# Two of the modulation's 24 column groups summed by TensorE instead of VectorE, with six slots for their pieces, and the first two groups of the output projection in turn

## The chip, the cores and the metric

One core of a Trainium2 chip runs the whole program. The metric is the device time of one execution in microseconds; the median of several runs is compared.

## The reference

Two decoder layers over a sequence of 256 tokens of width 2048, in f32 (`DEPTH` 2, `SEQ` 256, `D_FF` 5632). Each layer takes a modulation vector from `c`:

```
mod = (c_act @ ada_w[layer] + ada_b[layer])[:, None, :]
sh_m, sc_m, g_m, sh_f, sc_f, g_f = jnp.split(mod, 6, axis=-1)
h = rmsnorm(x, norm_mix[layer]) * (1 + sc_m) + sh_m
x = x + g_m * mix
h = rmsnorm(x, norm_ffn[layer]) * (1 + sc_f) + sh_f
x = x + g_f * swiglu(h, ffn_w_gate[layer], ffn_w_up[layer], ffn_w_down[layer])
```

In layer 0, `mix` is a projection of `h` to 5632 columns (`w_in`), 12 heads of dilated attention and four groups of a spatial gating unit (SGU) on it, and an output projection (`w_out`) of the 16 pieces. In layer 1 it is a short gated convolution between two projections. A final RMSNorm ends it.

`ada_w` is 2 x 2048 x 12288 f32. The product with it is a vector times a matrix: each of its 384 pieces of 512 KB is read once and used for one row of the result.

## The kernel before, in words

**Units.** All wide products run in 388 units: 0 to 43 the input projection, 44 to 59 the output projection, 60 to 191 the FFN of layer 0, then the convolution's and the second FFN. A unit is a 512x512 block of a weight matrix for both halves of the tokens: 24 matmuls of 512 columns. The weights come as two pieces of 512 KB (`raw`, slots: `RAW`). ScalarE rounds a piece to `whi` (L437), VectorE makes `wlo` = raw - whi (L730), and TensorE multiplies three times, high x whi, high x wlo, low x whi (`half_unit`, L1108 to L1110). There are four `whi`/`wlo` slots (`SPLIT`): ScalarE and VectorE work on the pieces of unit u+2 while TensorE runs unit u. The four banks 0 to 3 of PSUM hold the sums of two groups of units.

**The modulation.** `ADA` lists 24 groups of 1024 columns; the first four are quarters, 512 columns of shift and 512 of scale each. A group is 16 steps, one piece of `ada_w` each (128 rows, 1024 columns). In a step VectorE adds piece x `cact[:, k]` into one of two accumulators `acc` (`ada_op`, L756, for the first step L752, or L745 ahead of it); the 128 partitions are then summed by TensorE with a matrix of ones. For a shift or a scale that is `reduce_cols` (L1136), eight matmuls of one column with a 128x128 tile of `acc` as weights, and VectorE adds the bias (`keep_cols`). For a gate it is `reduce_row` (L1145).

**Order.** Every engine has its own queue in program order. `ada_to(u)` says up to which step the sum has come behind unit u: SyncE issues unit u+2's raw pieces and then that unit's ada pieces on one queue (`load_ada`, L367; `load_piece`, L354), and each load of ada waits until the step four before it has been done (`ADA_SLOTS`). VectorE runs the steps of unit u (`ada_ops`) behind the two `lo_piece` of that unit. The quarters are reduced behind units 8, 14 and 20 (`REDUCE_AT`), the other groups where `ADA_REDUCE` puts them. Behind a quarter, two blocks of the normalised x are transposed and scaled (`norm_turn`, `norm_quarter`), which the next part of the input projection needs: `VISITS` cuts that projection by quarters of its depth, so that its sums are kept in SBUF and added to by VectorE (`add_visit`, L912).

**Heads.** Between units 26 and 46, TensorE also runs the turns, scores and products of the heads (`SCORE_UNIT`, `QK_TURNS`); `heads_out` and `head_lo` put head m into `mixed` four units behind its scores. Units 44 and 45 take pieces 0 to 7 of `mixed` for the first group of output columns, unit 46 the SGU's pieces (waits for `sg_ready`), unit 47 the heads 8 to 11 (waits for `o_ready`); then the second, third and fourth group of columns follow, four units each. Each of these lines is in `OUT_ORDER` and at the end of the tensor block:

```
unit(46, G_OUT, 2, 4, mixed, sg_ready, lambda t: 2, 12)
heads_out(46)
reduce_ada(46)
unit(47, G_OUT, 3, 4, mixed, o_ready, lambda t: HEADS, 8)
```

Behind unit 59 the norm ahead of the FFN is made, whose shift and scale are the groups 6 to 9.

Of the kernel before, what the change touches and what calls it, by code (L numbers as in the profile page):

```python
# [37 lines left out]
RAW = 6  # L38
SPLIT = 4
ADA_SLOTS = 4  # L40
# [16 lines left out]
VISIT_AT = {u: v for u, (v, c, k) in enumerate(IN_UNITS) if k == VISITS[v][1][-1]}  # L57
LAST = {c: v for v, (c, ks) in enumerate(VISITS)}
BEFORE = {v: max((w for w in range(v) if VISITS[w][0] == c), default=None) for v, (c, ks) in enumerate(VISITS)}
KEPT = {c: n for n, c in enumerate((0, 3, 1, 4, 2, 5, 9, 10))}  # L60
UNIT_OF = {v: u for u, v in VISIT_AT.items()}
FIRST_OF = {k: min(u for u in range(44) if IN_UNITS[u][2] == k) for k in range(4)}
# [9 lines left out]
GROUP_END = [sum(GROUP_UNITS[:g + 1]) - 1 for g in range(len(GROUP_UNITS))]  # L72

# [11 lines left out]
ADA_OPS = KT * len(ADA)  # L85

ANGLES_AT, TRIG_AT = 3, 5
REDUCE_AT = {8: 1, 14: 2, 20: 3}
# [6 lines left out]
ROWS_TO = [sum(is_row(i) for i in range(j)) for j in range(len(ADA) + 1)]  # L95
COLS_TO = [j - ROWS_TO[j] for j in range(len(ADA) + 1)]
RED_TO = [j + ROWS_TO[j] for j in range(len(ADA) + 1)]


def cols_done(layer, which, n):  # L100
    return COLS_TO[ADA.index((layer, which, n))] + 1


def rows_done(layer, which, n):
    return 2 * ROWS_TO[ADA.index((layer, which, n))] + 2

# [44 lines left out]
TURNS = [[(t, q) for q in range(4) for t in range(2)]] + 4 * [((0, 0), (0, 1), (1, 0), (1, 1), (0, 2), (1, 2), (0, 3), (1, 3))]  # L151

SCORE_UNIT = (28, 29, 30, 33, 34, 35, 36, 37, 38, 39, 41, 42)
SCORE_AT = {u: n for n, u in enumerate(SCORE_UNIT)}
QK_TURNS = ((26, 0, 0, 0), (28, 0, 1, 0), (27, 0, 0, 1), (29, 0, 1, 1), (30, 1, 0, 0), (32, 1, 1, 0),
            (34, 1, 0, 1), (35, 1, 1, 1), (36, 2, 0, 0), (37, 2, 1, 0), (38, 2, 0, 1), (40, 2, 1, 1))
QK_TURNS = tuple(sorted(QK_TURNS))
QK_AT = {u: [b for b, q in enumerate(QK_TURNS) if q[0] == u] for u in range(46)}  # L160
QK_INDEX = {q[1:]: b for b, q in enumerate(QK_TURNS)}

# [5 lines left out]

OUT_ORDER = ((0, 1, 3, 2), (0, 1, 2, 3))
# [19 lines left out]
def decoder_kernel(nc, x_in, c_col, pos, ada_w, ada_b, g_mix, g_ffn, w_in, sgu_w, sgu_b, w_out,  # L191
                   conv_in, conv_w, conv_out, ff_gate, ff_up, ff_down, g_fin, freq_in, ident_in,
                   mask_in, out):
    with ExitStack() as ctx:
# [49 lines left out]
        junk = sb("junk", [P, 2, COLS], mybir.dt.bfloat16)  # L244
# [26 lines left out]
        Q_BANK, S_BANK, P_BANK, O_BANK, ADA_BANK = 4, 5, 6, 7, 7  # L271

# [7 lines left out]
        ada_step, ada_init, red_done, mod_done, row_done = sems("ada_step ada_init red_done mod_done row_done")  # L280
# [15 lines left out]
        N_CONST = 10  # L296

# [27 lines left out]
        def weight_pieces():  # L325
# [4 lines left out]
            for n in range(4):  # L330
                for k in OUT_ORDER[n > 0]:
                    for half in range(2):
                        yield piece_of(w_out_v, 2 * k + half, n)
# [14 lines left out]
        def _(sp):  # L348
# [7 lines left out]
            def load_ada(a):  # L356
                layer, which, n = ADA[a // KT]
                if a >= ADA_SLOTS:
                    sp.wait_ge(ada_step, a - ADA_SLOTS + 1)
                to, w = ada[:, a % ADA_SLOTS], ada_v[layer, :, a % KT, :]  # L360
                if a < QUARTERS * KT:
# [32 lines left out]
        def _(pool):  # L394
            def rope(i, kind):
                n = 2 * i + kind
                c = (Q, K)[kind][i]
                freed(pool, LAST[c], 0)
                freed(pool, LAST[c], 1)
# [11 lines left out]

            nc.gpsimd.memset(ones[:, :], 1.0).then_inc(pool_const, 1)
# [5 lines left out]
            for i in range(3):  # L418
                for kind in range(2):
                    rope(i, kind)  # L420
            for r, (g, n, t, on_ve) in enumerate(RES):
                if not on_ve:
                    freed(pool, g, t)
                    xs = x[:, t, COLS * n:COLS * n + COLS]
                    nc.gpsimd.tensor_tensor(xs, xs, tmp[:, r % 2, :], ALU.add).then_inc(x_pool, 1)  # L425
# [3 lines left out]
        def _(sa):  # L429
# [13 lines left out]
            def keep_row(u):  # L443
                for j, n in ADA_AT[u]:
                    if is_row(j):
                        half = ADA[j][2]
                        gate = ROWS_TO[j] // 2
# [3 lines left out]
                        sa.wait_ge(red_done, RED_TO[j] + n + 1)  # L451
# [35 lines left out]
            def norm_scaled(k, i, layer, sh):  # L487
# [122 lines left out]
            for n in range(46):  # L610
# [14 lines left out]
                for c in (SG_V, SG_U):  # L625
                    if n == UNIT_OF[LAST[c]] + 1:
                        freed(sa, LAST[c], 0)
                        freed(sa, LAST[c], 1)
# [36 lines left out]
            for n in range(2, 15):  # L665
# [61 lines left out]
        def _(ve):  # L727
# [9 lines left out]
            def ada_op(a):  # L737
                j, k = a // KT, a % KT
                layer, which, n = ADA[j]
                to, src, c = acc[:, j % 2, :], ada[:, a % ADA_SLOTS, :], cact[:, k:k + 1]  # L740
                if k == 0 and j >= 2:
                    ve.wait_ge(red_done, RED_TO[j - 1])
                if k == 0 and is_row(j):
# [5 lines left out]
                    ve.wait_ge(ada_init, ROWS_TO[j] + 1)  # L749
# [3 lines left out]
                else:  # L753
                    if k:
                        ve.wait_ge(ada_step, a)
# [7 lines left out]
            def keep_cols(j):  # L763
                layer, which, n = ADA[j]
                ve.wait_ge(red_done, RED_TO[j] + 1)
                if j < QUARTERS:
                    to, src = (v[:, :].rearrange("p (w f) -> p w f", f=KT)[:, SH_M:SC_M + 1, 4 * n:4 * n + 4]
                               for v in (mod, adab))
                    nc.vector.tensor_tensor(to, ps[:, ADA_BANK, COLS - 8:COLS].rearrange("p (w f) -> p w f", w=2), src,
                                            ALU.add).then_inc(mod_done, 1)  # L770
                else:
                    col = mod_column(layer, which, 8 * n)
# [656 lines left out]
```

## Time and profile before

| | |
|---|---|
| median of 3 runs | 2384.12 us (2381.06 to 2386.44) |
| the profiled execution | 2381.44 us, of it 2379.7 us from its first to its last instruction |
| TensorE (PE) busy | 2265.2 us, 95% |
| VectorE (DVE) busy | 1643.3 us, 69% |
| ScalarE (ACT) busy | 1056.7 us, 44% |
| DMA | 615.89 MB, mean 259 GB/s |
| mean granted clock of TensorE | 0.985 |

The profile's times are microseconds from the span's start. "Idle before, releaser" is the time an engine stood still ahead of an instruction, and what ended it. PEclk is the granted clock as a share of 2.4 GHz; 0.50 is the lower of its two levels, 1.2 GHz. The table of windows gives the busy time of each engine and, in brackets, its instructions.

### The profile page before, as it was taken

To read this page: it belongs to the slowest core of one execution; us is meant where nothing else is said; L and a number is where in the kernel's file an instruction comes from. 1 tells how busy PE (TensorE), PEld (TensorE's weight loads), DVE (VectorE), ACT (ScalarE), POOL (GpSimd) and SP (SyncE) were. 2 spreads that over 40 slices of the span, in tenths; PEclk is the share of its full clock that TensorE was granted. 3 is DMA by queue.
4 is the path that set the end of the run, shared out by engine and by line. 5 is a ranking of instruction groups with operands and counts; after the bars stand their busy time and mean duration, and the time that the engine had idled before them with its cause. 6 is when DMAs were issued, how large, how long until landed. Compare 5 with 4: busy or idle time off the path is not lost.

```text
span 2379.7 us, 26483 instructions
## 1 busy us (share of the span) xinstructions
PE 2265.2 (95%) x10172; PEld 1868.3 (79%) x10172; DVE 1643.3 (69%) x1618; ACT 1056.7 (44%) x1333; POOL 106.7 (4%) x71
## 2 busy tenths in 40 slices
PE   3988898989999999999999999998999999999998
PEld 2776677778888888888887888887888888888886
DVE  5898998977766777667777777687774454444554
ACT  4533454364444334444446444446444443444443
POOL 0002210100000010000010000010000001000010
PEclk9999999989999999999999999999999999999999
DMA  8897898968888888888886888886886666666663
GB/s 315 324 324 266 311 323 304 351 240 290 277 267 289 276 280 294 278 273 282 278 283 224 272 280 270 278 280 216 305 272 179 194 188 194 194 191 189 188 192 124
DMA packets 277838, 615.89 MB, mean 259 GB/s; under 512 B 19792, under 2 KB 20176, under 8 KB 277328
## 3 DMA queue, kind: packets, MB, share of 16 engines
q1 hardware_dynamic: 276272, 613.50, 77.4%
q8 instruction: 81, 1.33, 0.2%
q10 hardware_dynamic: 1440, 0.69, 0.1%
q14 instruction: 45, 0.37, 0.0%
HBM read 612.02 MB, written 2.10 MB: 258 GB/s over the span
## 4 chain that ended last, share of the span: by engine, by line
PE 81%; DVE 11%; issue 3%; DMA 3%; ACT 2%; SPq 0%; DVEq 0%; ACTq 0%
PE ps L1108 26%; PE ps L1109 26%; PE ps L1110 26%; DVE acc L756 5%; DVE wlo L730 3%; PE ps L1158 2%; DMA ada<-ada_w 2%; PE ps L1136 1%; DMA raw<-w_in 1%; DMA raw<-w_out 1%; ACT whi L437 1%; ACT hf L497 1%; DVE kept L912 1%; PE ps L1145 0%; DVE vtok L912 0%
## 5 line engine op out<-in xcount | busy, mean ns | idle before, releaser
L730 DVE TENSOR_TENSOR wlo<-raw,whi 128x1024 fp32r<-128x1024 f32 x776 | 957.6, 1237 | 645.5 <-ACT whi L437 645.4
L437 ACT ACTIVATE whi<-raw 128x1024 fp32r<-128x1024 f32 x776 | 823.2, 1062 | 1225.3 <-PE ps L1110 1053.2
L1108 PE MATMUL ps<-whi,h 128*128 128x512 f32 x2144 | 854.5, 399 | 21.9 <-issue 8.5
L1109 PE MATMUL ps<-wlo,h 128*128 128x512 f32 x2144 | 839.9, 392 | 0.0
L1110 PE MATMUL ps<-whi,h 128*128 128x512 f32 x2144 | 839.8, 392 | 0.0
L756 DVE SCALAR_TENSOR_TENSOR acc<-ada,cact,acc 128x1024 f32<-128x1024 f32 x368 | 486.4, 1322 | 23.0 <-DMA ada<-ada_w 12.2
L1108 PEld LDWEIGHTS ps<-whi,h 128*128 128x128 f32 x2144 | 406.1, 189 | 113.1 <-issue 18.9
L1109 PEld LDWEIGHTS ps<-wlo,h 128*128 128x128 f32 x2144 | 406.3, 190 | 85.4 <-issue 3.8
L1110 PEld LDWEIGHTS ps<-whi,h 128*128 128x128 f32 x2144 | 405.6, 189 | 86.2
L1108 PE MATMUL ps<-whi,act 128*128 128x512 f32 x704 | 274.7, 390 | 0.0
L1110 PE MATMUL ps<-whi,act 128*128 128x512 f32 x704 | 274.0, 389 | 0.0
L1109 PE MATMUL ps<-wlo,act 128*128 128x512 f32 x704 | 273.9, 389 | 0.0
L425 POOL TENSOR_TENSOR x<-x,tmp 128x512 f32<-128x512 f32 x40 | 70.8, 1793 | 1962.1 <-DVE tmp L847 1962.1
L1110 PEld LDWEIGHTS ps<-whi,act 128*128 128x128 f32 x704 | 132.1, 188 | 27.5
L1109 PEld LDWEIGHTS ps<-wlo,act 128*128 128x128 f32 x704 | 132.2, 188 | 27.3
L1108 PEld LDWEIGHTS ps<-whi,act 128*128 128x128 f32 x704 | 132.2, 188 | 27.2
L1108 PE MATMUL ps<-whi,mixed 128*128 128x512 f32 x256 | 103.7, 405 | 10.7 <-DVE wlo L730 5.4
L1109 PE MATMUL ps<-wlo,mixed 128*128 128x512 f32 x256 | 102.3, 400 | 0.0
L1110 PE MATMUL ps<-whi,mixed 128*128 128x512 f32 x256 | 102.0, 398 | 0.0
L1108 PEld LDWEIGHTS ps<-whi,mixed 128*128 128x128 f32 x256 | 49.7, 194 | 22.8 <-DVE wlo L730 7.1
L1158 PE MATMUL ps<-ident,xn 128*128 128x128 f32 x128 | 21.5, 311 | 42.6 <-ACT xn L484 42.6
L1110 PEld LDWEIGHTS ps<-whi,mixed 128*128 128x128 f32 x256 | 49.7, 194 | 10.8
(113 smaller groups left out, 842.5 us busy)
## 6 DMA issues: line engine op xcount, KB each, us to landing
ada<-ada_w SPq DMA_DIRECT2D x384, 512.0 KB, 5.6
raw<-ff_gate SPq DMA_DIRECT2D x176, 512.0 KB, 4.1
raw<-ff_up SPq DMA_DIRECT2D x176, 512.0 KB, 3.8
raw<-ff_down SPq DMA_DIRECT2D x176, 512.0 KB, 4.2
raw<-conv_in SPq DMA_DIRECT2D x96, 512.0 KB, 4.5
raw<-w_in SPq DMA_DIRECT2D x88, 512.0 KB, 6.8
raw<-w_out SPq DMA_DIRECT2D x32, 512.0 KB, 7.0
raw<-conv_out SPq DMA_DIRECT2D x32, 512.0 KB, 5.2
```

Of the source, the lines that this page charges most:

```text
L425: nc.gpsimd.tensor_tensor(xs, xs, tmp[:, r % 2, :], ALU.add).then_inc(x_pool, 1)
L437: nc.scalar.activation(whi[v % SPLIT][:, :, :], raw[:, v % RAW], ACT.Copy).then_inc(hi_ready, 1)
L497: nc.scalar.activation(hfs[k][:, i % 3, P * m:P * m + P], ps[:, 4 + i % 3, P * m:P * m + P], ACT.Identity, bias=mod[:, col:col + 1], scale ...
L730: nc.vector.tensor_tensor(wlo[v % SPLIT][:, :, :], raw[:, v % RAW], whi[v % SPLIT][:, :, :].bitcast(F32), ALU.subtract).then_inc(lo_ready, 1)
L756: nc.vector.scalar_tensor_tensor(out=to, in0=src, scalar=c, in1=to, op0=ALU.mult, op1=ALU.add)\
L912: nc.vector.tensor_tensor(of, ps[:, acc_bank(v, t), :], of, ALU.add).then_inc(acc_free[acc_bank(v, t)], 1)
L1108: nc.tensor.matmul(to, high, whi[v % SPLIT][:, k, :], start=begin, stop=False)
L1109: nc.tensor.matmul(to, high, wlo[v % SPLIT][:, k, :], start=False, stop=False)
L1110: ins = nc.tensor.matmul(to, low, whi[v % SPLIT][:, k, :], start=False, stop=end)
L1136: ins = nc.tensor.matmul(ps[:, ADA_BANK, COLS - 8 + n:COLS - 7 + n], acc[:, j % 2, P * n:P * n + P], ones[:, 0:1], start=True, stop=True)
L1158: return nc.tensor.transpose(to, src, ident[:, :])
```

## The change

The lines below are the core of the diff. `PE_GROUPS` are group 3 (the last quarter) and group 9 (the second half of the shift for layer 0's FFN).

```
-RAW = 6
+RAW = 5
-ADA_SLOTS = 4
+ADA_SLOTS = 6
+OUT_UNITS = ([(n, k) for ks in ((0, 1), (3, 2)) for n in range(2) for k in ks]
+             + [(n, k) for n in range(2, 4) for k in range(4)])
+PE_GROUPS = (3, 9)
+PE_LAG = 1
-REDUCE_AT = {8: 1, 14: 2, 20: 3}
+REDUCE_AT = {9: 1, 15: 2, 21: 3}
 def ada_to(u):
-    if u < 22:
-        return min(4 * KT, KT + (12 * (u + 1)) // 5)
+    if u < 9:
+        return 16 + 16 * (u + 1) // 9
+    if u < 21:
+        return 32 + 32 * (u + 1 - 9) // 12
     if u < U_F0 - 2:
-        return min(10 * KT, 4 * KT + (14 * (u - 21)) // 5)
-    return min(ADA_OPS, 10 * KT + u - (U_F0 - 3))
+        return min(10 * KT, 64 + 96 * (u + 1 - 21) // 36)
+    return min(len(OPS), 10 * KT + u - (U_F0 - 3))
...
+TURN_BANKS = ((5, 6), (4, 5, 6), (4, 5, 6), (4, 5, 6))
...
-        junk = sb("junk", [P, 2, COLS], mybir.dt.bfloat16)
+        junk = sb("junk", [P, COLS], mybir.dt.bfloat16)
...
+        def summed(engine, a):
+
+            j, k = OPS[a]
+            if j not in PE_GROUPS:
+                engine.wait_ge(ada_step, KT * VE_INDEX[j] + k + 1)
+            elif k < KT - 1:
+                engine.wait_ge(pe_step, (KT - 1) * PE_GROUPS.index(j) + k + 1)
+            else:
+                engine.wait_ge(red_done, RED_INDEX[j, 0] + 1)
...
             def load_ada(a):
-                    sp.wait_ge(ada_step, a - ADA_SLOTS + 1)
+                    summed(sp, a - ADA_SLOTS)
...
             def ada_op(a):
+                if j in PE_GROUPS:
+                    return
...
+            def ada_sums(u):
+
+                for a in range(ada_to(u - 1), ada_to(u)):
+                    j, k = OPS[a]
+                    if j not in PE_GROUPS:
+                        continue
+                    to = ps[:, SUM_BANK[j], 0:8]
+                    if k == 0:
+                        if j >= QUARTERS:
+                            pe.wait_ge(sg_ready, 2)
+                        nc.tensor.matmul(to, ident[:, :], columns_of(adab, j), start=True, stop=False)
+                    pe.wait_ge(ada_loaded[a % ADA_SLOTS], 16 * (a // ADA_SLOTS + 1))
+                    for n in range(8):
+                        ins = nc.tensor.matmul(to[:, n:n + 1], ada[:, a % ADA_SLOTS, P * n:P * n + P],
+                                               cact[:, k:k + 1], start=False, stop=k == KT - 1 and n == 7)
+                    ins.then_inc(red_done if k == KT - 1 else pe_step, 1)
...
             pe.wait_ge(const_loaded, 16 * N_CONST)
             norm_turn(0, 0)
+            reduce_cols(0)
             norm_turn(0, 1)
-            reduce_cols(0)
...
+            def out_unit(n):
+                m, k = OUT_UNITS[n]
+                ks = [q for i, q in OUT_UNITS if i == m]
+                ready, value = None, HEADS
+                if m == 0:
+                    ready = sg_ready if k == 3 else o_ready
+                    value = 2 if k == 3 else 4 * k + 4
+                unit(U_OUT + n, G_OUT + m, ks.index(k), 4, mixed, ready, lambda t: value, 4 * k)
...
+                ada_sums(n - PE_LAG)
```

A step of group 3 or 9 is now eight matmuls with a 128x128 tile of the piece itself as weights and one column of `cact` moving, added up in PSUM on top of the bias; no accumulator and no reduction follow, and VectorE only copies the eight columns. TensorE runs the steps of unit u behind unit u+1. Group 3 lies behind units 15 to 20, group 9 behind units 51 to 56. Of `SBUF`, one raw slot and one buffer of `junk` are given up for two ada slots. In the output projection, units 44 to 51 are now groups 0, 0, 1, 1, 0, 0, 1, 1, the SGU's pieces in unit 48 and the heads 8 to 11 in unit 49. The norm's first eight transposes use two banks instead of three. Steps done behind unit 20 are 64 in both; behind unit 28 they are 83 before and 85 now, behind unit 45 131 and 130, behind unit 50 145 and 144.

The first place is VectorE at units 15 to 18 (each line of `wlo` ends one half of a unit's work; `acc<-ada,cact,acc` are modulation steps). Before:

```order
L756 SCALAR_TENSOR_TENSOR acc<-ada,cact,acc 128x1024 x2
L730 TENSOR_TENSOR wlo<-raw,whi 128x1024
L912 TENSOR_TENSOR vtok<-ps,vtok 128x512 x2
L730 TENSOR_TENSOR wlo<-raw,whi 128x1024
L756 SCALAR_TENSOR_TENSOR acc<-ada,cact,acc 128x1024 x2
L730 TENSOR_TENSOR wlo<-raw,whi 128x1024
```

Now:

```order
L854 TENSOR_TENSOR h<-hf_51,h 128x4x128 x2
L779 TENSOR_TENSOR wlo<-raw,whi 128x1024
L953 TENSOR_TENSOR kept<-ps,kept 128x512 x2
L779 TENSOR_TENSOR wlo<-raw,whi 128x1024 x2
L953 TENSOR_TENSOR kept<-ps,kept 128x512 x2
L779 TENSOR_TENSOR wlo<-raw,whi 128x1024 x2
```

The steps between the `wlo` are gone; the additions of the visits (L953) stay.

The second place is TensorE (PE) behind unit 16, the end of its wide matmuls (L1158, L1159) and what stands ahead of unit 17, in the kernel now:

```order
L1158 MATMUL ps<-wlo,h 128x512
L1159 MATMUL ps<-whi,h 128x512
L1208 MATMUL ps<-adab,ident 128x8
L1211 MATMUL ps<-cact,ada 128x1 x16
L1227 MATMUL ps<-ident,xn_49 128x128 x8
L1157 MATMUL ps<-whi,h 128x512
```

The bias comes first (L1208), then the sixteen one-column matmuls of two steps. Before, unit followed unit there, and the one-column matmuls of a reduction stood once, behind unit 14:

```order
L1109 MATMUL ps<-wlo,h 128x512
L1110 MATMUL ps<-whi,h 128x512
L1136 MATMUL ps<-ones,acc 128x1 x8
L1108 MATMUL ps<-whi,h 128x512
L1109 MATMUL ps<-wlo,h 128x512
```

The third place is SyncE's queue at the start. Before:

```order
L369 DMA cact<-c_col 128x16
L367 DMA ada<-ada_w 128x2x512 x4
L372 DMA x<-x_in 128x2x2048
L367 DMA ada<-ada_w 128x2x512 x12
L354 DMA raw<-w_in 128x2x512 x6
```

Now:

```order
L411 DMA cact<-c_col 128x16
L409 DMA ada<-ada_w 128x2x512 x6
L414 DMA x<-x_in 128x2x2048
L409 DMA ada<-ada_w 128x2x512 x10
L395 DMA raw<-w_in 128x2x512 x6
```

Two more pieces stand ahead of x.

## Rows read from the trace of the kernel before

**Rows 1.** The page, part 1: busy time, share, instructions.

```profile
PE 2265.2 (95%) x10172; PEld 1868.3 (79%) x10172; DVE 1643.3 (69%) x1618; ACT 1056.7 (44%) x1333; POOL 106.7 (4%) x71
```

**Rows 2.** Windows, the rest of the span; columns as in rows 3.

```profile
495.00:2379.70 1884.70, 1859.05 (x8360) 1536.79 (x8360) 1224.41 (x1155) 835.20 (x977) 60.25 (x34) 0.99 0.75 244
```

**Rows 3.** Windows: width, busy PE, PEld, DVE, ACT, POOL, then PEclk, DMA share, GB/s.

```profile
45.80:99.80 54.00, 53.85 (x233) 44.07 (x233) 45.42 (x49) 31.03 (x45) 0.00 (x0) 1.00 0.87 312
99.80:147.30 47.50, 38.41 (x171) 30.89 (x170) 41.38 (x42) 22.60 (x32) 0.00 (x0) 0.96 0.94 340
147.30:194.10 46.80, 39.08 (x169) 32.10 (x170) 41.94 (x44) 17.18 (x23) 0.00 (x0) 0.90 0.91 317
194.10:255.80 61.70, 50.42 (x217) 40.32 (x218) 51.12 (x49) 23.50 (x30) 22.77 (x16) 0.94 0.73 256
255.80:393.00 137.20, 126.92 (x619) 104.25 (x617) 132.28 (x180) 76.88 (x150) 12.08 (x9) 0.99 0.91 318
393.00:429.90 36.90, 34.81 (x141) 28.98 (x142) 26.90 (x24) 9.99 (x13) 3.53 (x2) 0.86 0.77 272
429.90:468.70 38.80, 36.55 (x162) 29.70 (x160) 35.50 (x31) 13.97 (x16) 3.50 (x2) 0.96 0.99 376
468.70:499.70 31.00, 22.61 (x97) 17.79 (x97) 23.96 (x28) 14.61 (x25) 3.52 (x2) 0.87 0.85 316
```

**Rows 4.** PE in order of time: start, duration, line, idle before.

```profile
143.82 3.58 PE L1136 MATMUL ps<-ones,acc 128*128 128x1 f32 x16 [4.61 <-DVE acc L756]
...
190.69 3.57 PE L1136 MATMUL ps<-ones,acc 128*128 128x1 f32 x16 [6.02 <-DVE acc L756]
...
392.95 0.80 PE L1108 MATMUL ps<-whi,mixed 128*128 128x512 f32 x1 [5.27 <-DVE mixed L995]
...
400.05 0.59 PE L1235 MATMUL ps<-probT,vtok 128*128 128x256 f32 x2
...
402.95 3.45 PE L1136 MATMUL ps<-ones,acc 128*128 128x1 f32 x16 [2.09 <-DVE mixed L894]
...
486.75 0.49 PE L1108 MATMUL ps<-whi,mixed 128*128 128x512 f32 x1
```

**Rows 5.** DMA between 430 and 440 us.

```profile
DMA packets 1543, 4.05 MB, mean 405 GB/s; under 512 B 127, under 2 KB 127, under 8 KB 1543
```

**Rows 6.** PE, wide matmuls at full clock, and the eighth and ninth after 406.26.

```profile
774.21 0.39 PE L1108 MATMUL ps<-whi,h 128*128 128x512 f32 x1
774.43 0.39 PE L1109 MATMUL ps<-wlo,h 128*128 128x512 f32 x1
...
409.40 0.63 PE L1109 MATMUL ps<-wlo,mixed 128*128 128x512 f32 x1
409.82 0.46 PE L1110 MATMUL ps<-whi,mixed 128*128 128x512 f32 x1
```

**Rows 7.** The page, part 5: all of VectorE's modulation steps; busy, mean ns.

```profile
L756 DVE SCALAR_TENSOR_TENSOR acc<-ada,cact,acc 128x1024 f32<-128x1024 f32 x368 | 486.4, 1322 | 23.0 <-DMA ada<-ada_w 12.2
```

**Rows 8.** PE, one reduction at full clock, and wide matmuls behind reductions.

```profile
774.89 1.84 PE L1136 MATMUL ps<-ones,acc 128*128 128x1 f32 x16
776.59 0.49 PE L1108 MATMUL ps<-whi,act 128*128 128x512 f32 x1
...
147.26 0.77 PE L1108 MATMUL ps<-whi,h 128*128 128x512 f32 x1
...
406.26 0.77 PE L1108 MATMUL ps<-whi,mixed 128*128 128x512 f32 x1
```

**Rows 9.** DVE at the start, the step behind the load of x.

```profile
17.91 1.28 DVE L756 SCALAR_TENSOR_TENSOR acc<-ada,cact,acc 128x1024 f32<-128x1024 f32 x1 [5.50 <-DMA ada<-ada_w]
```

**Rows 10.** Windows at the start, columns as in rows 3.

```profile
24.00:28.00 4.00, 0.00 (x0) 0.00 (x0) 3.41 (x3) 0.00 (x0) 0.00 (x0) 1.00 0.87 275
```

**Rows 11.** Waits between 194 and 256 us: total, times, longest.

```profile
ACT whi L437 <- DMA raw<-w_in: 27.9, 10, 6.7
```

**Rows 12.** Windows around the fall of the clock, columns as in rows 3.

```profile
402.00:403.00 1.00, 0.05 (x1) 0.05 (x1) 0.90 (x2) 0.00 (x0) 0.00 (x0) 1.00 1.02 406
403.00:404.00 1.00, 1.00 (x6) 1.00 (x6) 0.00 (x0) 0.00 (x0) 0.00 (x0) 0.56 0.52 211
```

More of the change, by code:

```diff
@@ L296, in decoder_kernel, with columns_of, kept_of, whole @@
         N_CONST = 10
+        def summed(engine, a):
[6 more added lines that the diff above has]
+                engine.wait_ge(red_done, RED_INDEX[j, 0] + 1)
+        def columns_of(v, j):
+            layer, which, n = ADA[j]
+            if j < QUARTERS:
+                return v[:, :].rearrange("p (w f) -> p w f", f=KT)[:, SH_M:SC_M + 1, 4 * n:4 * n + 4]
+            col = mod_column(layer, which, 8 * n)
+            return v[:, col:col + 8]
+        def kept_of(c, t):
+            return kept[:, KEPT[c], t, :] if c in KEPT else vtok[:, t, COLS * (c - 6):COLS * (c - 5)]
+        def whole(engine, c):
+            for t in range(2):
+                freed(engine, LAST[c], t)
         def freed(engine, g, t):
@@ L329, in weight_pieces @@
                     yield piece_of(w_in_v, 2 * k + half, c)
[L330 to L333, printed above, removed]
+            for n, k in OUT_UNITS:
+                for half in range(2):
+                    yield piece_of(w_out_v, 2 * k + half, n)
             yield from feed_pieces(0)
@@ L417, in _ @@
             pool.wait_ge(trig_ready, 4)
[L418 to L425, printed above, removed]
+            for u in range(U_F0):
+                for i in range(3):
+                    for kind in range(2):
+                        if UNIT_OF[LAST[(Q, K)[kind][i]]] == u:
+                            rope(i, kind)
+                for r, (g, n, t, on_ve) in enumerate(RES[:8]):
+                    if not on_ve and GROUP_END[g] == u:
+                        residual(r)
+            for r in range(8, len(RES)):
+                if not RES[r][3]:
+                    residual(r)
         @block.scalar
@@ L669, in _ @@
                 keep_row(U_OUT + n)
-                if n % 4 == 1 and n > 4:
-                    square(R_OUT + 2 * (n // 4) - 2)
-                    square(R_OUT + 2 * (n // 4) - 1)
+                for m in range(3):
+                    if n == OUT_LAST[m] + 2:
+                        square(R_OUT + 2 * m)
+                        square(R_OUT + 2 * m + 1)
             norm(1, 0, SH_F, U_F0)
@@ L748, in ada_op @@
                         .then_inc(ada_init, 1)
-                    ve.wait_ge(ada_init, ROWS_TO[j] + 1)
+                    ve.wait_ge(ada_init, sum(is_row(i) for i in range(j)) + 1)
                 ve.wait_ge(ada_loaded[a % ADA_SLOTS], 16 * (a // ADA_SLOTS + 1))
@@ L895, in head_lo, with add_visit @@
                                             ALU.subtract).then_inc(o_ready, 1)
+            def add_visit(v):
+                for t in range(2):
+                    of = kept_of(VISITS[v][0], t)
+                    ve.wait_ge(acc_done, 2 * v + t + 1)
+                    freed(ve, BEFORE[v], t)
+                    nc.vector.tensor_tensor(of, ps[:, acc_bank(v, t), :], of, ALU.add).then_inc(acc_free[acc_bank(v, t)], 1)
             def gain_quarter(q):
@@ L1232, in heads_out @@
                     pe.wait_ge(mod_done, QUARTERS + cols)
-                    for t in range(2):
-                        freed(pe, LAST[V[m // 4]], t)
+                    whole(pe, V[m // 4])
                     nc.tensor.matmul(ps[:, O_BANK, 0:S], vtok[:, 0, P * m:P * m + P], probT[:, m % 2, 0:S],
@@ L1254, in _ @@
                 else:
-                    unit(n, G_OUT, n - 44, 4, mixed, o_ready, lambda t: 4 * (n - 44) + 4)
-                if n in REDUCE_AT:
+                    out_unit(n - 44)
+                ada_sums(n - PE_LAG)
+                if n in REDUCE_AT and REDUCE_AT[n] not in PE_GROUPS:
                     reduce_cols(REDUCE_AT[n])
```

180 lines of the change are left out of this document (93 added, 87 removed).

## The prediction

> **What bounds the kernel now.** I read the page first, then the table of eight stretches, then the instructions in order at the places where TensorE (PE) stood still, then the waits. Over the whole span PE is busy 95% [rows 1], and from 495 us on it has no hole worth naming: 1859 of 1884.7 us busy [rows 2]. There only a change of PE's own work could tell. The 500 us before are another kernel. I cut them where units of the first two projections begin, a unit being 24 wide matmuls, counted from the first at 45.84 us: units 0 to 8, 9 to 14, 15 to 20, 21 to 28, 29 to 45, 46 to 50, 51 to 56, and 57 to 59 with the norm's start [rows 3]. VectorE (DVE) is busy 41.4 of 47.5, 41.9 of 46.8 and 132.3 of 137.2 us there, PE 38.4, 39.1 and 126.9: both are nearly full, and DVE is what PE waits for. It waits 4.61, 6.02 us for a step of the modulation sum, and 5.27 and 2.09 us in units 46 and 47 for the last pieces of `mixed` [rows 4]. DMA moves 256 to 376 GB/s in these stretches; a window of 10 us shows 405 [rows 5]. So there are three resources, each within a fifth of the next.
>
> A wide matmul follows the one before by 0.227 us, so a unit is 24 x 0.227 = 5.44 us; at the clock's lower level (0.50) it follows by 0.42 to 0.43 [rows 6].
>
> **What the change moves.** 32 of the 160 modulation steps of this part (groups 3 and 9) leave DVE, at 1.322 us each [rows 7]: 42.3 us. PE takes each as eight one-column matmuls on a 128x128 f32 tile. No such accumulating run is in the trace, but the reduction of a summed group has the same shape: eight of them took 1.84 us at full clock and the next wide matmul began 1.70 us after their start; at half clock 3.44 us (143.82 to 147.26) [rows 4, 8]. I take 1.70 us: 16 x 1.70 = 27.2 us a group, 54.4 together, less two reductions (3.4) that fall away. Bounds of one step: nothing excludes that the sixteen loads overlap the wide matmul ahead better, which the 0.106 us between passes caps at some 1.5; above, 3.44.
>
> Where this lies matters more than the total. The order shows group 3 behind units 15 to 20 and group 9 behind units 51 to 56, two or three steps each time. There a PE unit becomes 5.44 + 2.67 x 1.70 = 10.0 us on the mean, while DVE is left with two `wlo` and at most two additions.
>
> Stretch by stretch, against the profiled run (481 us and the rest by its own span 2379.7, its time 2381.44):
> - *Start, to 45.84.* DVE stood 5.50 us for a piece behind x [rows 9] and 0.5 to 1.4 us four times more, 3.8 together, at 275 GB/s where 405 are to be had [rows 5, 10]. Six slots instead of four let SP issue two pieces more before x, and ask two steps earlier after it. I take 5 us off (0 to 8: all the stalls).
> - *Units 0 to 8.* PE is full. One reduction moves on to unit 9: -1.7.
> - *Units 9 to 14.* DVE's work is 41.4 plus one step, 42.7 against 47.5: -4.8.
> - *Units 15 to 20.* PE: 6 x 5.44 + 27.2 + 1.7 (a reduction) + 1.6 (sixteen transposes, an estimate from the sizes: 128 columns each, f32 twice, 0.1 us) = 63.1 against 46.8: +16.3.
> - *Units 21 to 28.* The new pace puts 21 steps here where 19 were, DVE 51.1 + 2.6 = 53.7, and I leave 2.3 of its 10.6 idle us: 56.0 against 61.7, -5.7. The idle hung on loads: ScalarE waited 27.9 us for `w_in` [rows 11]. SP is one queue, and a load of ada waits for the step four before it; with six slots that wait lies further back. Five slots of raw instead of six take a little of it away.
> - *Units 29 to 45.* DVE, 45 steps instead of 48: -3.9, and some 2 of waits: -6.
> - *Units 46 to 50.* With two groups in turn, the SGU pieces come in unit 48 and the last heads in unit 49, so the 5.27 and the 2.09 us and the half clock behind each go. Left is 5 x 5.44 + 1.8 (two heads, 0.9 each as at 400.05 [rows 4]) + 1.7 = 30.7 on PE, and 24 loads of 512 KB at 405 GB/s, 31.1: 31.5 against 36.9, -5.4.
> - *Units 51 to 56.* 6 x 5.44 + 27.2 + 1.7 = 61.5 against 38.8: +22.7.
> - *Units 57 to 59.* DVE and loads have had 20 us of slack, so PE runs through: 16.3 + the 7.5 us that the norm adds behind unit 59 (it began at 486.75 [rows 4], and 499.7 - 486.75 - 5.44 = 7.5) = 23.8 against 31.0: -7.2.
> - *After 499.7.* 328 units on PE; the raw loads come in early enough that no wait for them is in the list there, one slot less or not: 0.
>
> Sum: -5 -1.7 -4.8 +16.3 -5.7 -6 -5.4 +22.7 -7.2 = +3.2 us. DVE's 42 us and the slots buy 36, and PE takes 39. Cover: in both PE blocks the loads for the next units are hidden by PE; what is late next is PE itself.
>
> **The clock.** One term is missing. Behind a reduction at half clock the clock stayed at half: the passes ran from 402.95, the wide matmuls from 406.26, and still the eighth and the ninth of these stood 0.42 us apart, at 409.40 and 409.82, the ninth the first short one [rows 4, 6]. And it fell at 403, some 3 us after the wide matmuls had ended, though heads' matmuls stood in between [rows 4, 12]. A lone run of 1.84 us leaves it at full [rows 6, 8]. The new runs are 3.4 us (four) and 5.1 us (eight). If the clock falls in one, a last step costs 1.7 more and eight wide matmuls behind it 8 x 0.2 = 1.6: 3.3 us a fall. I take four of the twelve, half of the long ones: +13.2. Bounds 0 and 12 x 3.3 = 40.
>
> The Trainium skill, "TensorE: Matmul & The Clock Gate", Part 1, says that the throttled state is the default and that only array activity releases it, and Part 4 that transposes don't count as busy in the same way. Read that way, one-column passes, which are nearly all weight load, would not hold the clock in any of the runs; the trace agrees for the runs that began at half clock, and has none longer than 1.84 us that began at full. By the rule the sum would be +43, by the rows alone anything from +3.
>
> Forecast: 3.2 + 13.2 = +16.4 on the median of the runs, 2384.12 (the profiled run is 2.7 under it): 2400.5 us.
>
> **Rivals.**
> *PE's holes pay for it (faster).* In the eight stretches from 45.8 to 499.7 PE is busy 402.7 of 453.9 us: 51.2 are idle, exactly what the new work needs (54.4 - 3.4), and cold starts add some 12. If buffers (two units of wlo, six of ada, five of raw) let PE's full blocks and DVE's full blocks overlap, as they do if each engine can run two units off, all of it is filled: -12 - 5 at the start = -17, of which I take 15, 2369 us. It decides where units 21 to 50 take under 200 us in place of my 56.0 + 131.2 + 31.5 = 218.7. For: so many waits are for DVE or loads. Against: a DVE that ran ahead has only four whi/wlo slots, two units.
> *The clock falls in every run (slower still).* +3.2 + 40 = 2427 us. From what is said above.
> *A wash.* No fall at all, and +3.2: 2387 us; the reordering and the two buffers pay for PE's blocks.
> *The change doesn't do what it says:* excluded by the order rows; the steps are gone from DVE and the one-column matmuls are there.
> *Group 9 late.* Its columns (the shift of the next norm) are ready in unit 57, before the norm needs them behind unit 59; a fall on this needs PE to be 10 us behind its own order, which can't be. No chance given.
>
> **How the numbers follow.** Some clock falls, +10 to +25: 0.38. All or nearly all: 0.14. Wash, within 5 us: 0.18. Holes pay: 0.30. A change of 0.2% (4.8 us) is about what a measurement of this kernel can tell from none. Faster 0.30; same 0.16 (most of the wash); slower 0.54 (the first two and the rest of the wash). The range holds from the rival's 2369 to the all-falls 2427, with 2 us on the low side left in for noise of the median: 2367 to 2427. The likeliest case by itself is 2392 to 2410.
>
> **What would show it.** Right: PE units of about 10 us at 15 to 20 and 51 to 56, DVE idle there, one-column runs at 1.70 us a step, granted clock at 0.50 in parts of them; first wide matmul near 41; no 5 us hole in unit 46; start of the FFN near 503 plus the falls; from there the same 1880 us. Wrong: a step under 1.3 us on PE, the clock at 1.0 all through both blocks, or units 21 to 50 in less than 205 us.

## The result and the profile after

The changed kernel takes 2441.3 us (median of 4 runs, 2438.82 to 2442.1) against 2382.59 for the kernel before on the same chip: a ratio of 1.0244, 95% interval 1.0226 to 1.0262, 58.7 us slower. The profiled execution took 2440.86 us, 2439.1 of them its span. The forecast was slower, 2400.5, with a range up to 2427: the direction was right, the size was not, and the measured time lies outside the range.

The page, part 1, after (engine, busy us, share, instructions), against [rows 1]:

```profile
PE 2346.8 (96%) x10656; PEld 1946.6 (80%) x10656; DVE 1604.9 (66%) x1586; ACT 1058.4 (43%) x1333; POOL 106.7 (4%) x71
```

VectorE is busy 38 us less (the forecast moved 42.3), and TensorE 82 us more. The same stretches as in [rows 3], cut at the starts of the same units. Columns: stretch, width, busy time of PE, PEld, DVE, ACT, POOL, then PEclk, DMA share, GB/s.

```profile
0.00:42.90 42.90, 5.61 (x24) 4.84 (x24) 22.87 (x25) 15.99 (x33) 1.08 (x7) 1.00 0.90 324
42.90:94.30 51.40, 51.38 (x216) 42.13 (x217) 42.40 (x47) 33.33 (x47) 0.00 (x0) 1.00 0.96 348
94.30:137.30 43.00, 38.83 (x170) 31.51 (x170) 34.07 (x35) 20.66 (x29) 0.00 (x0) 0.92 0.93 323
137.30:221.80 84.50, 76.76 (x380) 67.13 (x378) 34.16 (x38) 18.53 (x24) 0.00 (x0) 0.76 0.60 202
221.80:288.10 66.30, 61.23 (x267) 50.66 (x267) 49.10 (x48) 23.72 (x30) 17.05 (x12) 0.87 0.77 260
288.10:421.30 133.20, 125.05 (x617) 102.25 (x615) 128.94 (x175) 73.71 (x149) 17.87 (x12) 1.00 0.93 324
421.30:451.10 29.80, 29.80 (x143) 24.97 (x141) 29.07 (x30) 10.87 (x13) 2.64 (x2) 1.00 0.98 366
451.10:523.00 71.90, 71.52 (x372) 63.11 (x371) 29.48 (x25) 16.45 (x21) 7.84 (x5) 0.80 0.74 252
523.00:558.70 35.70, 29.21 (x130) 24.23 (x130) 12.91 (x19) 12.61 (x23) 0.00 (x0) 0.79 0.36 118
558.70:2439.10 1880.40, 1857.38 (x8352) 1535.79 (x8352) 1221.88 (x1150) 832.55 (x969) 60.23 (x34) 0.99 0.75 244
```

| stretch | before | after | difference | forecast |
|---|---|---|---|---|
| start | 45.8 | 42.9 | -2.9 | -5 |
| units 0 to 8 | 54.0 | 51.4 | -2.6 | -1.7 |
| 9 to 14 | 47.5 | 43.0 | -4.5 | -4.8 |
| 15 to 20 | 46.8 | 84.5 | +37.7 | +16.3 |
| 21 to 28 | 61.7 | 66.3 | +4.6 | -5.7 |
| 29 to 45 | 137.2 | 133.2 | -4.0 | -6 |
| 46 to 50 | 36.9 | 29.8 | -7.1 | -5.4 |
| 51 to 56 | 38.8 | 71.9 | +33.1 | +22.7 |
| 57 to 59 and the norm's start | 31.0 | 35.7 | +4.7 | -7.2 |
| the rest | 1880.0 | 1880.4 | +0.4 | 0 |

The forecast column leaves out the clock, for which 13.2 us stood beside it. Read the PEclk column: it is 0.76 and 0.80 in the two stretches with the new work, 0.90 and 0.96 before. A unit with three steps behind it now takes 14.4 us; with 1.70 us a step it would be 5.44 + 5.10 = 10.5. These windows hold one such unit each:

```profile
181.90:196.30 14.40, 14.40 (x74) 12.68 (x74) 3.74 (x4) 2.12 (x2) 0.00 (x0) 0.74 0.47 160
483.20:497.60 14.40, 14.40 (x74) 12.81 (x74) 2.45 (x2) 2.12 (x2) 0.00 (x0) 0.74 0.61 190
```

PE is busy for the whole of them and VectorE for about a quarter or less. The clock falls inside the run of one-column passes. The run behind unit 21 began at 228.92, without a hole:

```profile
231.00:232.00 1.00, 1.00 (x11) 1.00 (x11) 0.43 (x1) 0.00 (x0) 0.00 (x0) 1.00 0.55 74
232.00:233.00 1.00, 1.00 (x7) 1.00 (x7) 0.00 (x0) 0.00 (x0) 0.00 (x0) 0.53 0.68 229
...
236.00:237.00 1.00, 1.00 (x4) 0.90 (x4) 0.64 (x3) 0.00 (x0) 0.00 (x0) 0.50 0.95 350
```

From 232 on 6 to 7 passes a us go through instead of 11, and the wide matmuls from 236.15 on start at the lower level too.

So it is in all eight runs of three steps. The four runs of two steps went through at full clock, some 3.5 us for both steps, and there the clock fell within 0.5 us of the run's end, in one of them 1.2 us behind it, in the one-column reduction that followed. One of the twelve falls, the one behind unit 16 at 163.8, may not be the steps' doing: without any group on TensorE (next section) the clock falls near the same place, at about 164. Every run of steps began at full clock.

ScalarE and VectorE now stand still for TensorE, which has not yet given back the `whi` and `wlo` of an earlier unit. Up to the FFN's first unit, before (0 to 500) and after (0 to 560), in total, times, longest:

```profile
ACT whi L437 <- PE ps L1110: 65.4, 28, 9.4
```

```profile
ACT whi L487 <- PE ps L1159: 230.3, 84, 13.3
```

### The profile page after: what moved, and what is told of

Its sections match the earlier page's. It is cut to its first block, busy times and chain, and to the rows that moved or that the text cites. A ratio compares the mean times of both kernels' runs of the same rounds, so it can differ in the third digit from the quotient of the medians.

```text
span 2439.1 us, 27386 instructions
## 1 busy us (share of the span) xinstructions
PE 2346.8 (96%) x10656; PEld 1946.6 (80%) x10656; DVE 1604.9 (66%) x1586; ACT 1058.4 (43%) x1333; POOL 106.7 (4%) x71
## 4 chain that ended last, share of the span: by engine, by line
PE 87%; DVE 8%; issue 3%; DMA 1%; ACT 1%; DVEq 0%; SPq 0%; ACTq 0%
PE ps L1157 27%; PE ps L1158 27%; PE ps L1159 27%; DVE acc L809 4%; PE ps L1211 3%; DVE wlo L779 2%; PE ps L1227 2%; PE ps L1189 1%; DMA ada<-ada_w 1%; DVE kept L953 0%; PE ps L1195 0%; DVE mx L1015 0%; ACT hf L547 0%; ACT whi L487 0%; DMA raw<-w_in 0%
## 5 line engine op out<-in xcount | busy, mean ns | idle before, releaser
L1158 PE MATMUL ps<-wlo,h 128*128 128x512 f32 x2144 | 845.3, 394 | 0.0
L1159 PE MATMUL ps<-whi,h 128*128 128x512 f32 x2144 | 844.6, 394 | 0.0
L1158 PEld LDWEIGHTS ps<-wlo,h 128*128 128x128 f32 x2144 | 409.4, 191 | 86.7 <-issue 3.8
L1159 PEld LDWEIGHTS ps<-whi,h 128*128 128x128 f32 x2144 | 408.8, 191 | 87.1
L809 DVE SCALAR_TENSOR_TENSOR acc<-ada,cact,acc 128x1024 f32<-128x1024 f32 x338 | 445.4, 1318 | 17.5 <-DMA ada<-ada_w 8.6
L1159 PE MATMUL ps<-whi,act 128*128 128x512 f32 x704 | 274.0, 389 | 0.0
L1158 PE MATMUL ps<-wlo,act 128*128 128x512 f32 x704 | 273.9, 389 | 0.0
L1159 PEld LDWEIGHTS ps<-whi,act 128*128 128x128 f32 x704 | 132.1, 188 | 27.6
L1158 PEld LDWEIGHTS ps<-wlo,act 128*128 128x128 f32 x704 | 132.2, 188 | 27.2
L1157 PE MATMUL ps<-whi,mixed 128*128 128x512 f32 x256 | 107.1, 418 | 0.4 <-DVE wlo L779 0.4
L1158 PE MATMUL ps<-wlo,mixed 128*128 128x512 f32 x256 | 104.9, 410 | 0.0
L1159 PE MATMUL ps<-whi,mixed 128*128 128x512 f32 x256 | 104.5, 408 | 0.0
L1211 PEld LDWEIGHTS ps<-cact,ada 128*128 128x128 f32 x512 | 70.4, 223 | 0.8
L1211 PE MATMUL ps<-cact,ada 128*128 128x1 f32 x512 | 69.5, 271 | 0.0
```

Of the source, the lines that this page charges most:

```text
L809: nc.vector.scalar_tensor_tensor(out=to, in0=src, scalar=c, in1=to, op0=ALU.mult, op1=ALU.add)\
L1157: nc.tensor.matmul(to, high, whi[v % SPLIT][:, k, :], start=begin, stop=False)
L1158: nc.tensor.matmul(to, high, wlo[v % SPLIT][:, k, :], start=False, stop=False)
L1159: ins = nc.tensor.matmul(to, low, whi[v % SPLIT][:, k, :], start=False, stop=end)
L1211: ins = nc.tensor.matmul(to[:, n:n + 1], ada[:, a % ADA_SLOTS, P * n:P * n + P], cact[:, k:k + 1], start=False, stop=k == KT - 1 and n == 7)
```

## The experiments

Every run was timed in three rounds against the kernel before on the same chip. The kernel before had medians of 2382.6, 2384.8, 2382.7 and 2382.4 us in the four sets, so a difference between runs of two sets is good to some 2 us.

### First set: take the parts apart

**No group on TensorE.** All else as changed.

```
-PE_GROUPS = (3, 9)
+PE_GROUPS = ()
```

> The changed kernel with no group on TensorE (PE_GROUPS empty): slots, pace, order of the output projection and reductions as changed, all 160 steps on VectorE. Theory A (the one-column runs, with the clock they lower, are the whole loss): the 12 long units go, and what is left are the gains of the slots and the order, 3 us at the start, 3 in units 0 to 8, 4 in units 29 to 45, 7 in units 46 to 50: about 2366 us, 2358 to 2376. Rival B (the pace, the slots or the later reductions cost something themselves): above 2390.

Measured: 2364.2 us, ratio 0.9921 (0.9901 to 0.9942). Theory A stands on this run, rival B falls: the 32 steps on TensorE cost 2441.3 - 2364.2 = 77.1 us, and the rest of the change gains 18.4.

**The steps spread.** The same 32 steps, one behind each quarter of a unit; `pe_step_of` is the body of `ada_sums` for one step.

```
 def unit(u, g, n, nu, of, ready=None, value=None, k0=None):
+    steps = pe_steps(u - PE_LAG)
     for half in range(2):
         for t in range(2):
...
             half_unit(u, g, t, n == 0, n == nu - 1, of, 4 * n if k0 is None else k0, half)
+            if steps:
+                pe_step_of(steps.pop(0))
```

> The changed kernel with the same steps on TensorE, but one at a time behind each quarter of a unit (1.7 us of one-column passes between 1.4 us of wide matmuls) instead of two or three in a row behind the unit. Theory A (only long unbroken runs lower the clock): granted clock 1.0 in the blocks, a unit 10.0 us on the mean instead of 14 with three steps, 12 units: 40 us less, about 2400 us. Rival C (what counts is the share of one-column work over a longer time, or the steps are slow for another reason, a wait for the pieces or the semaphores): the clock falls all the same, 2435 to 2445 or more.

Measured: 2406.4 us, ratio 1.0099 (1.0076 to 1.0122), 34.9 less than with the steps in a row. Two windows of two units with three steps each, and one step in order of time:

```profile
203.90:225.80 21.90, 21.90 (x147) 19.80 (x146) 7.67 (x8) 4.24 (x4) 0.00 (x0) 1.00 0.74 240
455.70:477.60 21.90, 21.90 (x147) 19.86 (x147) 5.14 (x6) 4.51 (x7) 0.00 (x0) 1.00 0.87 302
```

```profile
205.11 0.39 PE L1159 MATMUL ps<-whi,h 128*128 128x512 f32 x1
205.34 1.84 PE L1213 MATMUL ps<-cact,ada 128*128 128x1 f32 x16
207.04 0.49 PE L1157 MATMUL ps<-whi,h 128*128 128x512 f32 x1
```

The granted clock is 1.00 where it was 0.74, and two units with three steps each take 21.9 us instead of 28.8. The instructions are the same, so the 35 us are the clock's. The granted clocks say so too: 0.972 over 2439.1 us is some 68 us lost to the lower level, 0.987 over 2407.6 us some 31 (an estimate from spans and mean clocks). A step takes 1.70 us at full clock, as forecast; with the slower first wide matmul behind it a unit pays (10.95 - 5.44) / 3 = 1.84. Rival C falls as a forecast of this run; that the share of wide work counts is taken up in the third set. What is left, 2406.4 - 2364.2 = 42.2 us, is the price of the steps where the clock is mostly held.

Mostly, because in units 15 to 20 it was not. It had fallen at 147.4, in a hole of 5.53 us ahead of the reduction behind unit 15, and the first two spread steps began at the lower level:

```profile
148.78 3.58 PE L1195 MATMUL ps<-ones,acc 128*128 128x1 f32 x16 [5.53 <-DVE acc L809]
...
155.20 3.55 PE L1213 MATMUL ps<-cact,ada 128*128 128x1 f32 x16
...
161.32 3.41 PE L1213 MATMUL ps<-cact,ada 128*128 128x1 f32 x16
...
173.03 0.47 PE L1157 MATMUL ps<-whi,h 128*128 128x512 f32 x1 [3.10 <-issue]
```

The clock came back at 167.8, after 20.4 us, in the twelve wide matmuls that follow the second step. In the changed kernel, with 24 wide matmuls unbroken after the same reduction, it came back after some 10 (146.8 to 157.0). Six wide matmuls a step kept a full clock full; here, in the one case there is, they did not bring a low one back. The stretches from unit 15 on, cut at the starts of units 15, 21, 24, and of 51 and 58, the last to the FFN's first unit:

```profile
137.60:214.90 77.30, 68.67 (x380) 60.97 (x380) 33.13 (x36) 17.36 (x23) 0.00 (x0) 0.87 0.68 228
214.90:243.50 28.60, 24.30 (x130) 20.74 (x129) 19.70 (x22) 10.41 (x16) 0.00 (x0) 0.94 0.71 236
243.50:275.60 32.10, 30.23 (x140) 24.55 (x138) 31.07 (x29) 14.41 (x15) 17.06 (x12) 1.00 0.90 312
...
438.60:508.40 69.80, 69.41 (x443) 62.06 (x442) 31.37 (x26) 17.50 (x22) 6.92 (x5) 1.00 0.78 271
508.40:527.60 19.20, 13.03 (x57) 10.41 (x56) 11.59 (x18) 11.53 (x21) 0.00 (x0) 0.87 0.54 175
```

**The output projection's order alone**, on the kernel before: `OUT_UNITS`, `out_unit`, and the residuals and squares that hang on them, as in the change.

> The kernel before with only the output projection's first two groups in turn. Theory D (the waits of units 46 and 47 for the last heads and the SGU were on the path): 5.3 + 2.1 us of waits and some 3 us of half clock behind them go, 2374 to 2378 us. Rival E (VectorE is the bound there and only the place of the wait moves): within 2 us of before.

Measured: 2381.0 us, ratio 0.9993 (0.9984 to 1.0003): no difference that can be told, rival E. Unit 46 starts at 389.95 instead of 392.95, but until the next unit 15.6 us go by. The wait has only moved, to the reduction behind unit 46; the fourth set takes it away.

```profile
402.13 3.57 PE L1142 MATMUL ps<-ones,acc 128*128 128x1 f32 x16 [5.82 <-DVE mixed L899]
```

**The slots alone**, on the kernel before.

```
-RAW = 6
+RAW = 5
-ADA_SLOTS = 4
+ADA_SLOTS = 6
```

> The kernel before with only the slots changed: raw 5, ada 6, junk one buffer. Theory F (loads asked for earlier shorten the stalls on VectorE and ScalarE): 3 us at the start and 3 to 10 in units 9 to 45, 2370 to 2380 us. Rival G (one raw slot less makes up for it): within 2 us of before, or above.

Measured: 2369.8 us, ratio 0.9948 (0.9931 to 0.9966), 12.8 us less: theory F, at its upper end. ScalarE's waits for `w_in` between 194 and 256 us are 17.1 us instead of the 27.9 of [rows 11].

```profile
ACT whi L437 <- DMA raw<-w_in: 17.1, 6, 5.2
```

### Second set: where the 18 us come from, and the dear group

**Slots and order together**, on the kernel before.

> The kernel before with both the slots (raw 5, ada 6, one junk) and the output projection's first two groups in turn, nothing else. Alone they gave 12.8 us and 1.6 us. Theory H (the order only pays once the loads keep up: unit 45 to 51 took 31 to 44 us less in the run with everything but TensorE's groups): 2369.8 less 8 to 12, about 2359 us, under both kernels. Rival I (they add up as they stand, or share the same stalls): 2367 to 2371 us.

Measured: 2368.2 us, ratio 0.9934 (0.9919 to 0.9948). They do not add up to more than the slots: theory H falls.

**Early reductions.** The changed kernel with no group on TensorE, and the quarters' reductions of before together with the pace of the first 21 units that they need.

```
-    if u < 9:
-        return 16 + 16 * (u + 1) // 9
     if u < 21:
-        return 32 + 32 * (u + 1 - 9) // 12
+        return min(4 * KT, KT + (12 * (u + 1)) // 5)
...
-REDUCE_AT = {9: 1, 15: 2, 21: 3}
+REDUCE_AT = {8: 1, 14: 2, 20: 3}
```

> The changed kernel with no group on TensorE, and the pace of the first 21 units and the quarters' reductions as before (behind units 8, 14 and 20 instead of 9, 15 and 21). Theory J (a reduction one unit later leaves the norm's quarter no time before the unit that needs it, and PE waits at units 11, 17 and 23, with a cold clock behind): those units give back 10 to 15 us of 2364.2: about 2352 us. Rival K (the stalls only move, VectorE being the bound there): within 3 us of 2364.

Measured: 2357.7 us, ratio 0.9888 (0.9871 to 0.9904). It is 6.5 us under the run with late ones (7.9 by the two ratios), half of what theory J put on it, and beats the kernel before by 27. The mechanism is visible. In the run without groups on TensorE, which has the late reductions, units 11, 17 and 23 began behind holes of more than 3 us:

```profile
111.88 0.47 PE L1157 MATMUL ps<-whi,h 128*128 128x512 f32 x1 [3.59 <-issue]
...
164.20 0.77 PE L1157 MATMUL ps<-whi,h 128*128 128x512 f32 x1 [3.10 <-issue]
...
215.04 0.58 PE L1157 MATMUL ps<-whi,h 128*128 128x512 f32 x1 [3.10 <-issue]
```

With early ones none of these three is left; waits of 1.7, 1.7 and 2.7 us for `kept` stand elsewhere, so the gain is less than the sum of the holes. The profile names no releaser for the holes. In the changed kernel unit 11 starts at 111.69, just when VectorE has ended the first block of `h` that it reads, at 111.58, so that block is the likely one:

```profile
110.89 0.69 DVE L854 TENSOR_TENSOR h<-hf,h 128x512 fp32r<-128x512 f32 x1 [1.32 <-ACT h L553]
```

The reductions and their pace were changed together; how the 6.5 us divide between them stays open.

**Group 9 alone on TensorE.** `PE_GROUPS = (9,)` in the changed kernel.

> The changed kernel with group 9 alone on TensorE, group 3 back on VectorE. The whole loss of the two is 2441.3 - 2364.2 = 77 us. Theory A (16 steps at 1.75 us and a fall of the clock in each of six runs): half of it, 2364 + 34 to 42, about 2402 us. Rival L (group 3 is the dear one, because the norm's quarter hangs on it, and group 9 is cheap): under 2390 us.

Measured: 2405.4 us, ratio 1.0089 (1.0074 to 1.0104): 41.2 us over none, so 35.9 is left for group 3. Neither group is the dear one; rival L falls.

**Three banks for the turns.** `TURN_BANKS` as before, with no group on TensorE.

> The changed kernel with no group on TensorE and three banks for the first norm's transposes, as before, instead of two. Theory J (the late reduction, not the banks): within 2 us of 2364. Rival M (the second transpose of a pair waits for a bank): 3 to 8 us less.

Measured: 2363.2 us, ratio 0.9916 (0.9901 to 0.9930), 1.0 under the run with two banks: within the noise, rival M falls.

### Third set: what lowers the clock, and whether a group can pay

**Wide matmuls between the steps.** Group 9 in a row, and behind each step:

```
+                    for n in range(2):
+                        nc.tensor.matmul(ps[:, P_BANK, :], mixed[:, 0, 0:P], mixed[:, 0, :], start=True, stop=True)
```

> The changed kernel with group 9 alone on TensorE, its steps in a row behind the units as changed, but with two wide matmuls that nobody reads behind each step (0.45 us beside 1.8 us of one-column passes). Theory N (it is the unbroken run without a wide matmul that lowers the clock): granted clock 1.0 behind units 52 to 57, a unit with three steps 5.4 + 5.4 + 1.4 = 12.2 us instead of 14.4; 6 units give back 10 to 13 us of 2405.4: about 2394 us. Rival O (a fifth of wide work is too little; with half of it, as in the run with spread steps, the clock held): the clock falls as before and the added work comes on top, 2410 to 2418 us.

Measured: 2414.9 us, ratio 1.0132 (1.0117 to 1.0147). Theory N falls: the clock goes down all the same, in the second step of the run.

```profile
457.77 1.84 PE L1211 MATMUL ps<-cact,ada 128*128 128x1 f32 x16
459.47 0.72 PE L1215 MATMUL ps<-mixed 128*128 128x512 f32 x2
...
460.03 2.86 PE L1211 MATMUL ps<-cact,ada 128*128 128x1 f32 x16
462.75 1.20 PE L1215 MATMUL ps<-mixed 128*128 128x512 f32 x2
463.75 3.41 PE L1211 MATMUL ps<-cact,ada 128*128 128x1 f32 x16
```

```profile
457.00:460.00 3.00, 3.00 (x23) 2.77 (x22) 1.51 (x2) 1.06 (x1) 0.00 (x0) 1.00 0.00 0
460.00:463.00 3.00, 3.00 (x18) 2.97 (x17) 0.28 (x1) 0.00 (x0) 0.00 (x0) 0.60 0.59 180
463.00:466.00 3.00, 3.00 (x14) 2.81 (x14) 0.00 (x0) 0.00 (x0) 0.00 (x0) 0.50 0.64 185
```

So it is not enough to break the run, and the spread run's theory A, that only long unbroken runs lower the clock, does not hold in its letter either. Two wide matmuls a step (0.45 us) did not hold the clock, six (1.36 us) did; nothing in between was tried.

**Group 9 spread, in the best kernel.** The kernel with early reductions, group 9 on TensorE, one step a quarter.

> The best kernel so far (slots, order, early reductions, 2357.7 us) with group 9 on TensorE, its steps spread one by one over the quarters of units 52 to 57. Theory P (a step costs TensorE 1.8 us at full clock and saves VectorE 1.3 us where VectorE is not much later than TensorE): half of the 42 us between the run with spread steps and the one with none, 2357.7 + 21 = 2379 us. Rival Q (VectorE, relieved of 16 steps, lets the units after them run closer): 2350 to 2365 us.

Measured: 2378.9 us, ratio 0.9983 (0.9973 to 0.9992), 21.2 us over the same kernel without it. Theory P, which said 2379: even spread, a group on TensorE loses 21 us here.

### Fourth set: the order's wait

**The reduction of group 7 behind unit 47**, on slots and order.

```
-ADA_REDUCE[5:7] = (35, 36), (44,)
+ADA_REDUCE[5:8] = (35, 36), (44,), (47,)
```

> The kernel before with slots and order (2368.2 us), and the reduction of group 7 behind unit 47 instead of 46. It shares its bank with the heads, so behind unit 46 it waits for head 11, 5.2 us at 391.02, and the clock falls. Theory R (the reordered projection gained nothing because this reduction kept the wait): the hole goes, and with it the half clock, 7 to 10 us: about 2360 us. Rival S (the hole moves again, to unit 48 or to VectorE): 2366 to 2370 us.

Measured: 2359.7 us, ratio 0.9906 (0.9891 to 0.9921), 8.5 less than with it behind 46 (6.7 by the two ratios). Theory R. In the run with slots and order the hole stood ahead of that reduction:

```profile
391.02 3.58 PE L1142 MATMUL ps<-ones,acc 128*128 128x1 f32 x16 [5.20 <-DVE mixed L899]
```

It shares bank 7 with the heads and may not overwrite the last one. The change had moved both, the output units and this reduction: its placing rule puts the reduction behind unit 47, and no line of the diff says so. Moving the reduction alone, in the old order, was not tried, so it is open how much of the gain needs the new order.

**Three banks in the best kernel.**

> The best kernel so far (no group on TensorE, slots, order, early reductions, 2357.7 us) with three banks for the first norm's transposes. Theory (the bank cost 1.0 us, one place in units 12 to 13): 2356 to 2358 us. Rival (with early reductions the second bank is what the quarter waits for): 2350 to 2355 us.

Measured: 2357.8 us, ratio 0.9898 (0.9881 to 0.9914): no difference. The best kernel stays the one with early reductions, or this one.

## Why the prediction was right or wrong

**The direction, and the two blocks.** Right. The forecast said that TensorE becomes the bound behind units 15 to 20 and 51 to 56, that VectorE stands idle there, and that nothing moves in the 1880 us after. The first and the last are in the table, the second in the windows of 14.4 us.

**"I take four of the twelve, half of the long ones: +13.2."** This term failed. The clock fell in all eight runs of three steps and behind all four of two. At 196.29 to 207.72 a unit with two steps took 11.4 us where one with two spread steps takes 5.44 + 2 x 1.84 = 9.1. The unit with three steps took 14.4 where 10.9 is the price at full clock: 3.5 for each of eight and 2.3 for each of four is 37, and the medians say 35. The price of a fall was about right: 3.3 forecast, 2.9 by the medians. The rival "the clock falls in every run" was thus the mechanism, at 0.14; its 2427 us was still 14 us short, because of the sum below. Of [rows 12] I had made too little: there the clock fell while short matmuls and passes were running, and the single reduction of 1.84 us that leaves it at full says nothing of 3.4.

The Trainium skill, "TensorE: Matmul & The Clock Gate", Part 1, says that activity releases the throttle. Read as I had read it, with one-column passes not counting as activity, it gave the right side, and these runs agree with that reading: PE was busy for the whole 14.4 us of the units above, and its clock was 0.74.

**"Sum +3.2".** This failed too, by some 21 us: with the steps spread the change stands at 2406.4 - 2382.6 = +23.8. Most of that is one stretch.

- *"Units 15 to 20 ... = 63.1 us".* This sum is PE at full clock without a hole. One run of three steps lies behind unit 21 and not in here, so 58.0 was to be expected; the run with spread steps took 77.3. It has the holes of 5.53 and 3.10 us and the 20.4 us at the lower level, which cost some 10. I had moved the reduction of the second quarter into this stretch at 1.7 us and left out the wait ahead of it, 4.61 us in [rows 4], and the half clock that it leaves. In the changed kernel that wait is 5.56 us:

```profile
148.41 3.58 PE L1189 MATMUL ps<-ones,acc 128*128 128x1 f32 x16 [5.56 <-DVE acc L809]
```

- *"Units 9 to 14: -4.8".* The number came (-4.5), the reason did not: this was luck. I took VectorE as the bound, with 42.7 us of work; it was busy 34.1 of 43.0 us. What this stretch gained is the same reduction with its wait, which the next one paid.
- *"Units 21 to 28: -5.7" and "units 57 to 59: -7.2".* TensorE runs the steps one unit late, so one three-step run lies behind unit 21 and one behind unit 57; both were counted one stretch too early, which is no loss of its own. With the steps spread, units 21 to 28 took 28.6 + 32.1 = 60.7 us against 56.0 + 5.1, and units 51 to 59 with the norm's start 69.8 + 19.2 = 89.0 against 61.5 + 23.8 = 85.3. So both terms were sound; 16 x 0.14 = 2.2 us of the difference are what a slower wide matmul adds to each step.
- *What VectorE's relief buys.* The forecast had the 42 us and the slots buy 36. TensorE's own price at full clock is 32 x 1.84 less two reductions, 55.5 us, and 42.2 of it are in the time (no group against spread). So 42.3 us of VectorE's work taken away bought some 13, an estimate by difference, which has in it what the clock and the holes did. In the PE blocks VectorE has little to do with its freed time, because ScalarE and it work on unit u+2 and no further: ScalarE's waits for TensorE were 65.4 us before, 118.2 with the slots alone and 230.3 in the changed kernel. The four `whi`/`wlo` slots, which I gave as the ground against the rival "holes pay", held against my own sum as well.
- *Late reductions.* With their pace they cost 6.5 us, and the forecast had no term for them. I moved the reduction's own 1.7 us and did not ask who waits for it: the norm's quarter, its blocks of `h`, and the first unit that reads them, which had been three units behind the reduction and now is two. That is a wait which the forecast had at nothing. The changed kernel has holes of 3.59, 2.18 and 3.10 us at units 11, 17 and 23.

**The slots.** -5 at the start and waits in units 21 to 45 were forecast; the slots alone give 12.8 us (2.9 of it before unit 0). Right in kind; at the start only some 3 of the 5 came. The stall behind x, 5.50 us in [rows 9], did not go but is 6.54 now, and only the shorter ones went.

```profile
21.14 8.50 DVE L809 SCALAR_TENSOR_TENSOR acc<-ada,cact,acc 128x1024 f32<-128x1024 f32 x6 [6.54 <-DMA ada<-ada_w]
```

**The order of the output projection, "-5.4".** Right in the changed kernel (-7.1), for a reason that the forecast had only half: the order alone gives nothing that can be told, and with the slots it gave 8.5 us more once the reduction of group 7 no longer waited for head 11 in the same bank.

**"1.70 us a step".** Right: 1.84 busy, 1.70 to the next start, 3.4 at half clock. A unit pays 1.84 a step, with the slower wide matmul behind it.

## What to carry to other kernels

Before work is given to an engine that is already 95% busy, count what the engine it is taken from can do with the time, through the slots between them: here 42 us freed were worth some 13. Matmuls that move one column, eight in 1.70 us, did not hold TensorE's clock here, in a row or with two wide ones behind every eight; with six it held. Spread them thinly between wide ones if they must be there, price the wide ones behind them too, and see that they begin at full clock. When a wait is moved with its work into another stretch, move its length too. And a change in several parts is worth taking apart: this one held some 25 us of gain (slots, order with its reduction) and lost it under 77 us of steps, with 6.5 more in the later reductions.

## What the hardware did that I had not expected

TensorE's granted clock fell to 0.50 with the engine busy 100% of the time and no hole before it, 3 us into a run of one-column f32 passes (228.92 to 232). It fell even with two 512-column matmuls behind each eight one-column ones, and held at 1.00 through 20 us and more with six; but six did not bring it back when it was low already, for 20.4 us (147.4 to 167.8 in the spread run). The passes themselves run at half speed then, 3.4 instead of 1.70 us for sixteen, though a pass moves a single column. The weight loads (PEld) are busy 1.00 of the time in these windows as well, and one takes 192 ns on the mean at full clock (229.5 to 231.5) and 333 at the lower level (232.5 to 235.5); that the loads set the pace is likely, and not shown. What lies between the two mixtures was not tried.
